# Dense feed-forward with up and gate units as seven block products, and modulation units 1024 columns wide

## The chip, the cores and the metric

The kernel runs on one core of one Trainium2 chip, in float32 throughout. The metric is the device time of one execution in microseconds (us). Engines are named as in the profile: PE is TensorE (matmuls), PEld its weight loads, DVE is VectorE, ACT is ScalarE, POOL is GpSimd, SP is SyncE, whose queue issues nearly all transfers.

## What is computed

256 tokens of width 1024 go through two layers of a first block (a mixer of three branches, then a feed-forward: dense in layer 0, eight experts in layer 1) and two layers of a second block. The change touches the dense feed-forward of layer 0 and the modulation vectors:

```python
D_MODEL, SEQ, D_FF = 1024, 256, 2816

def _swiglu(h, w1, w3, w2):
    return (jax.nn.silu(h @ w1) * (h @ w3)) @ w2

cond = jax.nn.silu(c)                       # 1024 numbers
for l in range(DEPTH):
    mod = cond @ w_mod[l] + b_mod[l]        # 6 vectors of 1024: sh1, sc1, g1, sh2, sc2, g2
    ...
    h = _modulate(_rmsnorm(x, norm2_w[l]), sh2, sc2)
    y = _swiglu(h, ffn_w1[i], ffn_w3[i], ffn_w2[i])    # layer 0
    x = x + g2[:, None, :] * y
```

## The kernel before

**Units and ring.** All weights come as a stream of units of 1 MB (128 partitions x 2048 numbers) into a ring of 11 slots in SBUF. SP issues the loads in the order of the stream; before each it waits until the unit that lay in that slot has been used: `unit_done` counts for units that PE uses, `part_done` for modulation units that DVE uses (L1400). A wait there holds back all later loads.

**Groups.** The 2816 hidden columns are 11 groups of 256 (`FG`, g = 0 to 10). PE's `swiglu` (L899) does, in group g >= 1: a `w1` unit and a `w3` unit through `columns_unit` (L492), each into one PSUM bank, transposed: 2 column blocks x 8 contraction blocks, with 128x128 of the weights stationary and all 256 tokens (`hT`) moving. Then `down(g - 1)` (L901) multiplies the hidden values of the group before by the `w2` unit into banks 4 to 7, which hold the sum of all groups. In some groups `mod_spread` (L575) follows, which turns a finished modulation vector. Group 0 goes through `lead_units` (L524), which works on the two token tiles apart, as their normed columns `hT` come in, with 128 tokens moving. Last comes group 10, with its own order.

**ACT** takes the `w1` bank through Silu into `gate_h[g % 2]` (L1781). **DVE** (`hidden`, L2526) multiplies that by the `w3` bank into `actT[g % 2]`, which PE's `down` needs. After it in its queue come, in group 0, `angles()` (L2074: masks and rotary angles for the second block, nothing near needs them), and in group g >= 1 the modulation units of `FFN_PARTS[g - 1]` (4 in group 1, 3 in groups 2 to 9), and `mod_spread` where a vector is complete. Every DVE instruction waits for the one before it (`link`).

**Banks.** `next_bank("U")` alternates banks 0 and 1, `next_bank("T")` banks 2 and 3. `free(bank)` makes PE wait until the last reader of that bank is done. 39 units have gone through "U" when group 0 starts, so its `w1` unit lies in bank 1 (read by ACT) and its `w3` unit in bank 0 (read by DVE).

**A modulation unit** is 1024 rows x 256 columns of `w_mod`. DVE's `row_product` (L2138) makes one `tensor_scalar` and seven `scalar_tensor_tensor` of 128x256 for it: acc = w * cond[k] + acc. Four units fill the 1024 columns of `PART[n % 2]`. 12 such units are spread over the mixer of layer 0 and 28 over the dense feed-forward.

**An existing scheme.** The mixer of layer 1 and the last stage already compute some 512-wide units with seven products instead of eight (`summed_product`, L1081): sums of weight blocks (DVE, `first_sums_in_place` and others) and of token blocks (`token_sums`, L2751), seven products, and partial results added on DVE (`added`, L2192). `SUMMED` says who reads each product.

Of the kernel before, what the change touches and what calls it, by code (L numbers as in the profile page):

```python
# [15 lines left out]
P = 128  # L16
# [178 lines left out]
def two_blocks(nc, stream, cols_d, rows_d, bgate_d, x_d, pos_d, out_d, stop=None):  # L195
# [3 lines left out]
    part_units = {(l, j): u for u, (name, l, j) in enumerate(names) if name == "part"}  # L199
    lead_at = {j: u for u, (name, l, j) in enumerate(names) if name == "lead"}  # L200
# [5 lines left out]
    with ctx:  # L206
# [173 lines left out]

        def by_k(a):
            return a.rearrange("p (k c) -> p k c", c=WC)

        D_T1 = [by_k(ring[:, RING_DSW, i * 2 * WC:(i + 1) * 2 * WC]) for i in range(2)]
# [15 lines left out]
        flatY = YT[:, :, :, :].rearrange("p b h s -> p (b h s)")  # L400
# [18 lines left out]
        def _(pe):  # L419
# [478 lines left out]

            def swiglu(l):  # L899

                def down(g, s=None, only=None):  # L901
                    if s is None:
                        s = landed_unit()
                    need(("w3", l, g))
                    for t in range(T) if only is None else only:
# [13 lines left out]
                for g in range(FG):  # L919
# [3 lines left out]
                    columns_unit("act", ("w1", l, g))  # L923
                    columns_unit("dve", ("w3", l, g))
                    if g < FG - 1:
                        down(g - 1)
                        for _ in FFN_PARTS[g - 1]:
                            skip_unit()
                        for part in parts_by[g]:
                            mod_spread(*part)  # L930
                        continue
# [627 lines left out]
        def _(act):  # L1559
# [221 lines left out]
            def swiglu(l):  # L1781
                for g in range(FG):
                    rows_out(("w1", l, g), gate_h[:, g % 2, :].rearrange("p (t c) -> p t c", t=T), ACT.Silu)
                    if g == 1:
                        angles()
# [203 lines left out]
        def _(dve):  # L1989
# [141 lines left out]
            def mod_part(l, j):  # L2131
# [4 lines left out]
                row_product(part_units[l, j], PART[n % 2][:, (j % 4) * UC:(j % 4 + 1) * UC])  # L2136
# [389 lines left out]
            def hidden(l, turn=None, dense=False, e=None):  # L2526
                for g in range(FG):
                    taken(("w1", l, g), turn)
                    b = bank_of(dve, ("w3", l, g), turn)
                    if dense:  # L2530
                        tt(actT[:, g % 2, :, :], view(b, 2, S), gate_h[:, g % 2, :].rearrange("p (k s) -> p k s", k=2),
                           ALU.mult, c=took)
                    else:
                        tt(actT_e[:, g % 3, :, :], view(b, 2, CAP), gate_e[:, g % 2, :, :], ALU.mult, c=took)
                    if dense and g == 0:
                        angles()
                    if dense and g == 1:
                        dve.wait_ge(*from_act.more())
# [21 lines left out]
                    if dense and g >= 1:  # L2560
                        for p in FFN_PARTS[g - 1]:
                            mod_part(*p)
                        for p in parts_by[g]:
                            mod_spread(*p)
# [123 lines left out]
            def ffn(l):  # L2688
                if l == 0:
                    hidden(l, dense=True)  # L2690
# [357 lines left out]
def lay_out(inp):  # L3048
# [9 lines left out]
    for u, (name, l, j) in enumerate(units):  # L3058
        if name in ("mod", "part", "lead"):
# [79 lines left out]
```

## Time and profile before

| | |
|---|---|
| three timed runs | 2308.69, 2308.86, 2311.12 us; median 2308.86 |
| profiled execution | 2313.64 us, of which span 2311.9 us |
| granted TensorE clock, mean over the span | 0.993 |
| PE busy | 2242.4 us (97% of the span) |
| DVE busy / ACT busy | 983.0 us (43%) / 478.6 us (21%) |
| dense feed-forward of layer 0 | about 397 to 640 us of the span |

A row of the timeline merges instructions of one form; a matmul of the program shows as two MATMUL and two LDWEIGHTS instructions, so that a `columns_unit` of 16 matmuls is 32. The duration of one MATMUL is longer than the distance to the next, since they overlap: PE's pace is the stretch divided by the count. "Idle before <- releaser" is the time in which the engine had nothing running, and what ended it. PEclk is the granted clock as a share of 2.4 GHz, 0.5 being 1.2 GHz.

### The profile page before, as it was taken

The page shows a single profiled execution, that of the slowest core. Times are in us where ns is not written, and L with a number is a line of the kernel's source. Part 1 is how long each engine was busy: PE and PEld are TensorE (multiplying, and loading weights), DVE is VectorE, ACT ScalarE, POOL GpSimd, SP SyncE. Part 2 cuts the span into 40 slices and gives each one's busy share as a digit, 9 for nine tenths or more (in the row PEclk, how much of TensorE's full clock was granted, in tenths as well). Part 3 has the DMA queues.
Part 4 walks back from the last instruction along what each step waited for, and adds up shares of the span by engine and source line. Part 5 has one row for each costly group of instructions (what it writes and reads, how often), then busy time and mean ns, then how long its engine had stood idle before and what let it go on. Part 6 is the DMA issues. An engine that isn't in the chain of part 4 may idle for free.

```text
span 2311.9 us, 48423 instructions
## 1 busy us (share of the span) xinstructions
PE 2242.4 (97%) x21380; PEld 1646.3 (71%) x21380; DVE 983.0 (43%) x2016; ACT 478.6 (21%) x889; POOL 26.7 (1%) x66
## 2 busy tenths in 40 slices
PE   8999999999999999989999999999999999999998
PEld 6888767777668876677877778777768874444544
DVE  3675642655563665331121121121123444475663
ACT  2343311000025332110000000000012431233343
POOL 2000000000000000000000000000000000000000
PEclk9999999999999999999999999999999999999999
DMA  9553255677533333549999999999982313343330
GB/s 377 191 215 141 91 218 201 241 287 304 205 128 128 130 127 125 212 175 399 401 403 408 395 403 399 397 408 401 408 328 110 110 64 137 127 146 124 114 109 19
DMA packets 75526, 537.96 MB, mean 233 GB/s; under 512 B 8552, under 2 KB 8560, under 8 KB 11440
## 3 DMA queue, kind: packets, MB, share of 16 engines
q1 hardware_dynamic: 72864, 526.14, 58.5%
q0 software_dynamic: 1360, 4.85, 0.6%
q8 instruction: 172, 2.82, 0.5%
q10 hardware_dynamic: 1088, 3.81, 0.4%
q14 instruction: 42, 0.34, 0.0%
HBM read 529.91 MB, written 4.85 MB: 231 GB/s over the span
## 4 chain that ended last, share of the span: by engine, by line
PE 91%; DVE 5%; ACT 3%; issue 1%; DMA 0%; DVEq 0%; ACTq 0%; SPq 0%
PE ps L956 21%; PE ps L487 11%; PE ps L476 11%; PE ps L1107 10%; PE ps L520 7%; PE ps L980 7%; PE ps L988 4%; PE ps L795 4%; PE ps L910 3%; PE ps L820 2%; PE ps L1210 2%; PE ps L564 2%; PE ps L1150 1%; PE ps L1341 1%; PE ps L1124 1%
## 5 line engine op out<-in xcount | busy, mean ns | idle before, releaser
L956 PEld LDWEIGHTS ps<-hT,ring 128*64 128x64 f32 x11264 | 474.5, 138 | 45.9 <-issue 41.5
L956 PE MATMUL ps<-hT,ring 128*64 128x96 f32 x11264 | 484.9, 247 | 6.2 <-DVEq L2742 4.2
L2007 DVE TENSOR_TENSOR RA<-ps,RA 128x192 f32<-128x192 f32 (+1 forms) x111 | 47.4, 427 | 665.3 <-PE ps L956 550.5
L1570 ACT ACTIVATE RA<-ps 128x192 f32<-128x192 f32 (+2 forms) x159 | 69.8, 439 | 1117.7 <-PE ps L956 574.4
L487 PE MATMUL ps<-hT,ring 128*128 128x256 f32 (+1 forms) x1280 | 269.0, 370 | 0.1
L476 PE MATMUL ps<-ring,hT 128*128 128x256 f32 x1184 | 262.0, 381 | 0.0
L487 PEld LDWEIGHTS ps<-hT,ring 128*128 128x128 f32 x1280 | 232.0, 190 | 33.1 <-issue 3.1
L476 PEld LDWEIGHTS ps<-ring,hT 128*128 128x128 f32 x1184 | 222.9, 190 | 31.7 <-issue 2.0
L520 PE MATMUL ps<-ring,hT 128*128 128x256 f32 x736 | 168.6, 384 | 2.0 <-DVE hT L2007 1.7
L980 PE MATMUL ps<-ring,RA 128*64 128x512 f32 x704 | 167.7, 594 | 0.1
L520 PEld LDWEIGHTS ps<-ring,hT 128*128 128x128 f32 x736 | 139.4, 193 | 22.6 <-issue 2.2
L1570 ACT ACT_TABLE_LOAD x86 | 110.3, 1283 | 55.4 <-DVE small L2013 28.2
L2007 DVE TENSOR_TENSOR ring<-ring 128x1024 f32<-128x1024 f32 (+3 forms) x101 | 106.1, 1050 | 25.3 <-ACT ring L1570 22.2
L1107 PE MATMUL ps<-ring,hT 128*128 128x512 f32 x216 | 97.5, 603 | 0.0
L988 PE MATMUL ps<-ring,RA 128*32 128x256 f32 x1408 | 85.9, 382 | 0.0
L980 PEld LDWEIGHTS ps<-ring,RA 128*64 128x64 f32 x704 | 46.4, 137 | 53.1 <-issue 53.1
L988 PEld LDWEIGHTS ps<-ring,RA 128*32 128x32 f32 x1408 | 40.8, 109 | 60.9 <-issue 38.9
L795 PE MATMUL ps<-ring,YT 128*128 128x512 f32 x192 | 83.1, 592 | 0.0
L1570 ACT ACTIVATE RB<-ps 128x512 f32<-128x512 f32 x60 | 35.8, 597 | 227.4 <-PE ps L476 94.5
L2016 DVE SCALAR_TENSOR_TENSOR QT<-ring,cond,QT 128x256 f32<-128x256 f32 x161 | 78.1, 485 | 5.8
L910 PE MATMUL ps<-ring,RA 128*128 128x512 f32 x176 | 77.5, 592 | 0.0
L1107 PEld LDWEIGHTS ps<-ring,hT 128*128 128x128 f32 x216 | 41.1, 193 | 49.6 <-issue 48.9
(327 smaller groups left out, 2164.8 us busy)
## 6 DMA issues: line engine op xcount, KB each, us to landing
ring<-stream SPq DMA_DIRECT2D x497, 1024.0 KB, 8.9
slots_scratch<-YT ACTq DMA_DIRECT2D x7, 384.0 KB, 8.4
x_rows<-x SPq DMA_DIRECT2D x2, 512.0 KB, 12.4
gates_row<-bgate SPq DMA_DIRECT2D x1, 1024.0 KB, 16.7
QT<-bgate SPq DMA_DIRECT2D x1, 1024.0 KB, 19.1
rows_scratch<-RB ACTq DMA_DIRECT2D x2, 512.0 KB, 4.7
out<-x_rows SPq DMA_DIRECT2D x2, 512.0 KB, 2.6
rowt<-rows SPq DMA_DIRECT2D x1, 460.0 KB, 14.1
```

The lines of the kernel that those rows point to most:

```text
L476: m = pe.matmul(ps[:, b, t * UC:(t + 1) * UC], lhs[:, k, t * P:(t + 1) * P], ring[:, s, k * UC:(k + 1) * UC], start=k == 0, stop=k == KC - 1)
L487: m = pe.matmul(ps[:, b, c * w + t * P:c * w + (t + tiles) * P], ring[:, s, k * UC + c * P:k * UC + (c + 1) * P], hT[:, k, t * P:(t + tile ...
L520: m = pe.matmul(ps[:, b, t * UC:(t + 1) * UC], hT[:, k, t * P:(t + 1) * P], ring[:, s, k * UC:(k + 1) * UC], start=k == 0, stop=k == KC - 1)
L795: m = pe.matmul(ps[:, b + t, :], YT[:, br, k, t * P:(t + 1) * P], ring[:, s, k * 512:(k + 1) * 512], start=k == 0, stop=k == 3)
L910: m = pe.matmul(ps[:, 4 + 2 * t + n, :], actT[:, g % 2, k, t * P:(t + 1) * P], ring[:, s, k * D + n * 512:k * D + n * 512 + 512], start=g ...
L956: m = pe.matmul(ps[64 * j:64 * (j + 1), b, c * CAP:(c + 1) * CAP], ring[:, s, k * UC + c * P + 64 * j:k * UC + c * P + 64 * (j + 1)], hT[: ...
L980: pe.matmul(ps[64 * j:64 * (j + 1), 4, :], actT_e[:, g % 3, k, 0:WIDE], ring[:, s, k * D + 512 * j:k * D + 512 * (j + 1)], **flags(g, k))
L988: m = pe.matmul(ps[32 * j:32 * (j + 1), 5, 0:256], actT_e[:, g_ % 3, k, WIDE:CAP], ring[:, s_, k * D + 256 * j:k * D + 256 * (j + 1)], **f ...
L1107: m = pe.matmul(ps[:, b, :], lhs, rhs, start=k == 0 and i in (0, 1, 3), stop=k == KH - 1, skip_group_check=i not in (0, 1, 3))
L1570: return nc.scalar.activation(out, in_, func, **kw)
L2007: link(v.tensor_tensor(out, a, b, op), c)
L2016: link(v.scalar_tensor_tensor(out, a, s_, b, op0, op1), c)
```

## The change

Three things change in the dense feed-forward, groups 1 to 10, and one in all modulation units of the kind `part`.

1. `columns_unit` is replaced by `column_product`. With the weights of a unit as 2x2 blocks (512 rows x 128 columns each) and the tokens as 2x2 blocks (128 tokens x 512), the four blocks of the result come from seven products (Winograd's form), i = 0 to 6, of 4 matmuls each, 128x128 stationary and 128 tokens moving. The `w1` and the `w3` unit take turns: product i of `w1`, product i of `w3`, product i + 1 of `w1` and so on. `w1` uses banks 0 and 1, `w3` banks 2 and 3; products 0, 2, 4, 6 go to the first bank of each and 1, 3, 5 to the second, most adding to what is there, so that each product waits until the result before it in its bank has been read.
2. DVE makes the sums: `token_sums("ffn")` once (4 `tensor_tensor` of 128x512), `column_sums` for the `w1` and the `w3` unit of each group (4 of 128x512 each, as soon as the last product of the group before is done), and adds three products per unit to the result (`added`, 128x128). ACT copies the other four products of each unit out of PSUM, and its Silu then works in place in SBUF.
3. DVE's order: per group g >= 1: `added` 1 (both units), from group 2 on one modulation unit, `added` 4 and 5, `column_sums(g + 1)`, the hidden product, `mod_spread`, in group 1 `angles()`, then the remaining modulation units (4 in group 1, 2 later). In group 0: token sums, column sums of group 1, hidden product.
4. A `part` unit is now 256 rows x 1024 columns, and DVE makes two instructions of 128x1024 for it instead of eight of 128x256.

```diff
@@ PE, column_product and swiglu @@
+            def column_product(key, s, b0, i):
+
+                b = b0 + (i in (1, 3, 5))
+                free(b)
+                if i == 2:
+                    pe.wait_ge(*sums.more())
...
+                for k in range(KH):
...
+                    m = pe.matmul(ps[:, b, 0:P], w[:, k, :], rhs, start=k == 0 and i in (0, 1, 3),
+                                  stop=k == KH - 1, skip_group_check=i not in (0, 1, 3))
...
-                    columns_unit("act", ("w1", l, g))
-                    columns_unit("dve", ("w3", l, g))
...
+                    at = [(name, landed_unit()) for name in ("w1", "w3")]
+                    for i in range(len(SUMMED)):
+                        for n, (name, s) in enumerate(at):
+                            column_product((name + "p", l, g), s, 2 * n, i)
+                    taken_by("act", [], ("w1", l, g))
+                    taken_by("dve", [], ("w3", l, g))
...
+                    if g < FG - 1:
+                        down(g - 1, s0, [0])
+                        for part in parts_by[g]:
+                            mod_spread(*part)
+                        down(g - 1, s0, [1])
+                        continue
@@ ACT, swiglu @@
+                for g in range(1, FG):
+                    for i, t, c in ((0, 0, 0), (2, 0, 1), (3, 1, 1), (6, 1, 0)):
+                        for name, dst in (("w1", gate_h), ("w3", F_UP)):
+                            b = bank_of(act, ((name + "p", l, g), i))
+                            link(fn(dst[:, g % 2, c * S + t * P:c * S + (t + 1) * P], ps[:, b, 0:P], ACT.Copy), took)
+                    taken((("w1p", l, g), 5))
+                    link(fn(gate_h[:, g % 2, :], gate_h[:, g % 2, :], ACT.Silu), took)
@@ DVE, mod_part @@
-                row_product(part_units[l, j], PART[n % 2][:, (j % 4) * UC:(j % 4 + 1) * UC])
+                s, fill, _ = plan[part_units[l, j]]
+                dve.wait_ge(landed[s], 16 * fill)
+                for i in range(2):
+                    k = j % 4 * 2 + i
+                    w = ring[:, s, i * D:(i + 1) * D]
+                    if k == 0:
+                        ts(PART[n % 2], w, cond[:, 0:1], None, ALU.mult)
+                    else:
+                        stt(PART[n % 2], w, cond[:, k:k + 1], PART[n % 2], ALU.mult, ALU.add, c=part if i else step)
@@ DVE, swiglu @@
+                def column_sums(name, g):
+                    s, fill, _ = plan[ffn_at[name, g]]
+                    dve.wait_ge(landed[s], 16 * fill)
+                    if g > 1:
+                        bank_of(dve, ((name + "p", l, g - 1), 6))
+                    t3, t2, t1, t4 = F_T[name]
+                    tt(t3, block_of(s, 1, 1), block_of(s, 0, 1), ALU.subtract)
+                    tt(t2, t3, block_of(s, 0, 0), ALU.add)
+                    tt(t1, block_of(s, 1, 1), t2, ALU.subtract)
+                    tt(t4, block_of(s, 1, 0), t2, ALU.subtract, c=sums)
...
+                for g in range(1, FG):
+                    parts = FFN_PARTS[g - 1]
+                    for name in ("w1", "w3"):
+                        added(name, g, 1, 0, 0, 0)
+                    if g > 1:
+                        for p in parts[:1]:
+                            mod_part(*p)
+                    for i, t, c, first in ((4, 1, 1, 3), (5, 0, 1, 2)):
+                        for name in ("w1", "w3"):
+                            added(name, g, i, t, c, first)
+                    if g < FG - 1:
+                        for name in ("w1", "w3"):
+                            column_sums(name, g + 1)
...
+                    hidden_of(g)
+                    for p in parts_by[g]:
+                        mod_spread(*p)
+                    if g == 1:
+                        angles()
+                    for p in parts[int(g > 1):]:
+                        mod_part(*p)
```

PE at the start of group 1, before: the last matmuls of group 0, then the two units (in the rows, `landed3` and `landed7` stand for the arrival of the units, `act_took` and `dve_took` for a bank read by ACT or DVE).

```order
L487 MATMUL ps<-hT,ring 128x128 x24
L487 MATMUL ps<-hT,ring 128x256 [waits act_took,landed3]
L487 MATMUL ps<-hT,ring 128x256 x15
L487 MATMUL ps<-hT,ring 128x256 [waits dve_took,landed7]
L487 MATMUL ps<-hT,ring 128x256 x15
```

And after, the first products of group 1; `sums_made` stands for the column sums.

```order
L500 MATMUL ps<-hT,ring 128x128 x24
L924 MATMUL ps<-hT,ring 128x128 [waits dve_took,landed7,landed3]
L924 MATMUL ps<-hT,ring 128x128 x3
L924 MATMUL ps<-hT,ring 128x128 [waits act_took]
...
L924 MATMUL ps<-hT,ring 128x128 [waits dve_took]
L924 MATMUL ps<-hT,ring 128x128 x3
L924 MATMUL ps<-YT,RA 128x128 [waits sums_made,act_took]
...
L924 MATMUL ps<-YT,RB 128x128 [waits sums_made,act_took]
...
L924 MATMUL ps<-YT,RA 128x128 [waits dve_took]
```

The first matmul of group 1 waited for a bank that ACT reads; now it waits for the bank that DVE's hidden product of group 0 reads.

DVE from the last `hT` columns to the first modulation unit, before.

```order
L2013 TENSOR_SCALAR hT<-ps,A,modc 128x128 [waits dve_took] x3
L2007 TENSOR_TENSOR RA<-ps,RA 128x512 [waits unit_done,act_took,dve_took]
L2077 TENSOR_SCALAR idx<-idx 128x256 [waits dve_took]
...
L2013 TENSOR_SCALAR sinr<-sinr 128x16 [waits dve_step]
L2007 TENSOR_TENSOR RA<-ps,RA 128x512 [waits unit_done,act_took,dve_gave_act]
L2011 TENSOR_SCALAR QT<-ring,cond 128x256 [waits burst_for_dve,landed9,act_gave_dve,dve_took]
L2016 SCALAR_TENSOR_TENSOR QT<-ring,cond,QT 128x256 [waits dve_step] x7
```

And after: from the last `hT` columns to the first partial result of group 1.

```order
L2053 TENSOR_SCALAR hT<-ps,A,modc 128x128 [waits dve_took] x3
L2047 TENSOR_TENSOR YT<-hT 128x512 [waits act_took,dve_took]
...
L2047 TENSOR_TENSOR RA<-ring 128x512 [waits landed3,dve_step]
L2047 TENSOR_TENSOR RA<-RA,ring 128x512 [waits dve_step]
L2047 TENSOR_TENSOR RA<-ring,RA 128x512 [waits dve_step] x2
L2047 TENSOR_TENSOR RB<-ring 128x512 [waits landed7,sums_made]
L2047 TENSOR_TENSOR RB<-RB,ring 128x512 [waits dve_step]
L2047 TENSOR_TENSOR RB<-ring,RB 128x512 [waits dve_step] x2
L2047 TENSOR_TENSOR RA<-ps,RA 128x512 [waits unit_done,act_took,sums_made]
L2047 TENSOR_TENSOR RA<-ps,RA 128x128 [waits act_took,burst_for_dve,dve_took]
```

The hidden product of group 0 (`RA<-ps,RA 128x512`) came right behind the columns; now four token sums and eight column sums stand ahead of it.

DVE at the end of group 1 and the start of group 2, after.

```order
L2047 TENSOR_TENSOR RA<-YT,RA 128x512 [waits act_took,sums_made]
L2117 TENSOR_SCALAR idx<-idx 128x256 [waits dve_took]
...
L2053 TENSOR_SCALAR sinr<-sinr 128x16 [waits dve_step]
L2051 TENSOR_SCALAR QT<-ring,cond 128x1024 [waits landed9,burst_for_dve,dve_gave_act]
L2056 SCALAR_TENSOR_TENSOR QT<-ring,cond,QT 128x1024 [waits dve_step]
...
L2056 SCALAR_TENSOR_TENSOR QT<-ring,cond,QT 128x1024 [waits landed5,part_done]
L2056 SCALAR_TENSOR_TENSOR QT<-ring,cond,QT 128x1024 [waits dve_step]
L2047 TENSOR_TENSOR RA<-ps,RA 128x128 [waits act_took,burst_for_dve,part_done]
```

The first partial result of group 2 that DVE reads (`RA<-ps,RA 128x128`) stands behind `angles()` and eight instructions of 128x1024; before, the hidden product of a group was the only one for which PE's next steps waited.

## Rows read from the trace of the kernel before

**Rows 1.** The page: busy time, and the chain that ended last.
```profile
PE 2242.4 (97%) x21380; PEld 1646.3 (71%) x21380; DVE 983.0 (43%) x2016; ACT 478.6 (21%) x889; POOL 26.7 (1%) x66
...
PE 91%; DVE 5%; ACT 3%; issue 1%; DMA 0%; DVEq 0%; ACTq 0%; SPq 0%
```

**Rows 2.** Windows, groups 1 to 10: length, busy (count) per engine, PEclk, DMA, GB/s.
```profile
413.60:630.70 217.10, 217.10 (x943) 158.23 (x943) 124.81 (x280) 7.89 (x14) 0.00 (x0) 1.00 0.69 273
```

**Rows 3.** Chain, groups 0 to 4: start us, us, what, instructions.
```profile
397.56 7.14 PE ps L487 x64
...
434.48 13.81 PE ps L487 x64
448.29 6.87 PE ps L910 x16
455.16 1.72 PE ps L581 x4
...
498.24 1.03 PE ps L587 x32
```

**Rows 4.** Timeline, PE, the start of `down(0)`: start us, us, instruction.
```profile
427.45 7.03 PE L910 MATMUL ps<-ring,RA 128*128 128x512 f32 x16
```

**Rows 5.** Groups of instructions with shapes apart, DVE and ACT: busy us, mean ns.
```profile
L2016 DVE SCALAR_TENSOR_TENSOR part_sum<-ring,cond,part_sum 128x256 f32<-128x256 f32 x140 | 67.9, 485 | 5.0
L2011 DVE TENSOR_SCALAR RB<-x_rows,small 128x1024 f32<-128x1024 f32 x12 | 9.0, 754 | 0.4
L2007 DVE TENSOR_TENSOR ring<-ring 128x512 f32<-128x512 f32 x12 | 8.3, 692 | 0.6 <-ACT ring L1570 0.2
L2016 DVE SCALAR_TENSOR_TENSOR ring<-ring 128x1024 f32<-128x1024 f32 x2 | 2.5, 1226 | 5.0 <-ACT ring L1570 5.0
L2120 DVE SCALAR_TENSOR_TENSOR junk<-ps,ident 128x128 f32<-128x128 f32 x10 | 2.9, 291 | 5.1 <-PE ps L610 4.8
```

**Rows 6.** Timeline, ACT and DVE around group 0, and layer 1's token sums.
```profile
405.68 1.93 ACT L1570 ACTIVATE hT<-ps,modc,A 128x128 f32<-128x128 f32 x4 [4.90 <-PE ps L564]
...
414.66 0.29 DVE L2077 TENSOR_SCALAR idx<-idx 128x256 int32<-128x256 int32 x1
...
422.74 0.17 DVE L2013 TENSOR_SCALAR sinr<-sinr 128x16 f32<-128x16 f32 x1
427.75 0.69 DVE L2007 TENSOR_TENSOR RA<-ps,RA 128x512 f32<-128x512 f32 x1 [4.83 <-PE ps L487]
...
650.36 0.69 DVE L2007 TENSOR_TENSOR part_sum<-hT 128x512 f32<-128x512 f32 x1 [0.70 <-ACT hT L1570]
651.08 0.69 DVE L2007 TENSOR_TENSOR part_sum<-part_sum,hT 128x512 f32<-128x512 f32 x1
```

**Rows 7.** Windows of 7 us, each from PE's first matmul after a wait.
```profile
269.40:276.40 7.00, 6.94 (x24) 6.04 (x25) 3.55 (x11) 4.22 (x9) 0.00 (x0) 0.60 0.02 7
635.90:642.90 7.00, 6.98 (x29) 4.76 (x30) 3.95 (x6) 1.83 (x4) 0.00 (x0) 1.00 0.00 0
...
865.90:872.90 7.00, 6.96 (x30) 6.17 (x31) 3.53 (x11) 4.22 (x8) 0.00 (x0) 0.79 0.03 11
1006.90:1013.90 7.00, 6.98 (x108) 6.98 (x110) 0.00 (x0) 0.33 (x1) 0.00 (x0) 0.62 0.05 15
```

**Rows 8.** Timeline, PE: the waits ahead of these windows [idle before <-releaser].
```profile
269.46 1.22 PE L769 MATMUL ps<-ring 128*128 128x256 f32 x2 [1.80 <-ACT ring L1570]
...
635.92 1.09 PE L564 MATMUL ps<-ident,RB 128*128 128x128 f32 x8 [1.83 <-DVE RB L2011]
...
865.93 1.22 PE L769 MATMUL ps<-ring 128*128 128x256 f32 x2 [1.80 <-ACT ring L1570]
...
1006.92 9.28 PE L956 MATMUL ps<-hT,ring 128*64 128x96 f32 x158 [4.15 <-DVEq L2742]
```

**Rows 9.** Windows, the mixer of layer 0 and after it.
```profile
80.00:120.00 40.00, 39.49 (x204) 33.96 (x203) 31.38 (x74) 17.21 (x40) 0.00 (x0) 1.00 0.63 237
120.00:160.00 40.00, 38.56 (x189) 32.63 (x188) 31.51 (x63) 16.49 (x26) 0.00 (x0) 1.00 0.62 237
```

More of the change, by code:

```diff
@@ L199, in two_blocks @@
     part_units = {(l, j): u for u, (name, l, j) in enumerate(names) if name == "part"}
+    ffn_at = {(name[:2], g): u for u, (name, _, g) in enumerate(names) if name in ("w1f", "w3f")}
     lead_at = {j: u for u, (name, l, j) in enumerate(names) if name == "lead"}
@@ L379, in two_blocks, with by_f, block_of @@
                 "mix": [S_TOP[:, 0], S_TOP[:, 1], S_MIX[:, 0], S_MIX[:, 1]]}
+        flatY = YT[:, :, :, :].rearrange("p b h s -> p (b h s)")
+        def by_f(a):
+            return a.rearrange("p (k c) -> p k c", k=KH)
+        def block_of(s, kh, c):
+            return ring[:, s, kh * KH * UC:(kh + 1) * KH * UC].rearrange("p (k c) -> p k c", k=KH)[:, :, c * P:(c + 1) * P]
         def by_k(a):
             return a.rearrange("p (k c) -> p k c", c=WC)
+        S_FFN = flatY[:, 0:2048].rearrange("p (i k s) -> p i k s", i=4, k=KH)
+        S_OF["ffn"] = [S_FFN[:, i] for i in range(4)]
+        F_UP = flatY[:, 2048:3072].rearrange("p (n c) -> p n c", n=2)
+        F_T = {name: [by_f(R[:, i // 2, 1024 + i % 2 * WC:1024 + (i % 2 + 1) * WC]) for i in range(4)]
+               for name, R in (("w1", RA), ("w3", RB))}
         D_T1 = [by_k(ring[:, RING_DSW, i * 2 * WC:(i + 1) * 2 * WC]) for i in range(2)]
@@ L2524, in mixer, with swiglu, added, hidden_of @@
                 project(f"m{l}o", f"n2{l}", A2_l[l], modc_l[l][:, 24:32], gates_l[l][:, 0, :])
-            def hidden(l, turn=None, dense=False, e=None):
+            def swiglu(l):
+                def added(name, g, i, t, c, first):
+                    key = (name + "p", l, g)
+                    b = bank_of(dve, (key, i))
+                    taken((key, first))
+                    a = (gate_h if name == "w1" else F_UP)[:, g % 2, c * S + t * P:c * S + (t + 1) * P]
+                    tt(a, ps[:, b, 0:P], a, ALU.add, c=took)
+                def column_sums(name, g):
[8 more added lines that the diff above has]
+                    tt(t4, block_of(s, 1, 0), t2, ALU.subtract, c=sums)
+                def hidden_of(g):
+                    taken(("w1", l, g))
+                    up = view(bank_of(dve, ("w3", l, g)), 2, S) if g == 0 else F_UP[:, g % 2, :].rearrange("p (k s) -> p k s", k=2)
+                    tt(actT[:, g % 2, :, :], up, gate_h[:, g % 2, :].rearrange("p (k s) -> p k s", k=2), ALU.mult, c=took)
+                taken((f"n2{l}", 1, 1))
+                token_sums("ffn")
+                for name in ("w1", "w3"):
+                    column_sums(name, 1)
+                hidden_of(0)
+                for g in range(1, FG):
[9 more added lines that the diff above has]
+                    if g < FG - 1:
+                        for name in ("w1", "w3"):
+                            column_sums(name, g + 1)
+                    if g == 3:
+                        dve.wait_ge(*from_act.more())
+                    hidden_of(g)
[5 more added lines that the diff above has]
+                        mod_part(*p)
@@ L2527, in hidden @@
+            def hidden(l, turn=None, e=None):
                 for g in range(FG):
@@ L2529, in hidden @@
                     b = bank_of(dve, ("w3", l, g), turn)
[L2530 to L2538, printed above, removed]
+                    tt(actT_e[:, g % 3, :, :], view(b, 2, CAP), gate_e[:, g % 2, :, :], ALU.mult, c=took)
                     if turn is not None and g == 0:
@@ L2689, in ffn @@
                 if l == 0:
-                    hidden(l, dense=True)
+                    swiglu(l)
                     mod_bias(1, 0, A1_l[1], "n1")
@@ L3058, in lay_out @@
     for u, (name, l, j) in enumerate(units):
-        if name in ("mod", "part", "lead"):
+        if name == "part":
+            stream[u] = unit_of(w_mod[l][j % 4 * 2 * P:(j % 4 + 1) * 2 * P], j // 4 * D, D)
+        elif name in ("mod", "lead"):
             stream[u] = unit_of(w_mod[l], j * UC)
```

34 lines of the change are left out of this document (14 added, 20 removed).

## The prediction

> **What bounds the kernel now.** I read the page first: PE is busy for 97% of the span and 91% of the chain that ended last is PE [rows 1]. The table of stretches over groups 1 to 10 of the dense feed-forward shows more than that: 217.10 us, in all of which PE is busy at a clock of 1.00, while DVE works 124.81 us and ACT 7.89 us [rows 2]. So in this stage only PE's own work counts, and every wait that the change puts into it adds in full. The chain cuts the stage up: two units take 13.81 us (64 instructions), `down` 6.87 us, a spread 1.72 or 1.03 us [rows 3]. The ten groups repeat this.
>
> **PE's work.** A pair of units now costs 14 products of 4 matmuls, 112 instructions with 128 tokens moving. The trace has this form: the lead of group 0 took 7.14 us for 64, 0.1116 us each [rows 3]. So a pair costs 112 x 0.1117 = 12.51 us instead of 13.81, saving 1.30 us, and ten pairs save 13.0 us. One eighth of the columns goes, but a matmul half as wide costs a little more than half: 0.1116 against 13.81 / 64 / 2 = 0.108 us. That half, 0.108, bounds the pace from below, with a saving of 17.2 us; I take 0.1117, from 64 instructions of exactly this form. It is the bound from above too: that lead had satisfied waits between its matmuls, as the products have, and they are in its pace.
>
> The Trainium skill ("TensorE: Matmul & The Clock Gate", section "Wait — 56ns, not 53.3ns?") gives a matmul a small fixed cost beside its columns, the same at every width. By its 2.5 ns, off 0.2158 us and added again after halving, the narrow pace would be 0.109 us (an estimate) and the saving 16 us. The lead shows 0.1116 [rows 3], about twice that fixed cost, and the sum goes by the lead.
>
> **DVE's new work, per group.** Column sums: 8 x 0.725 us (0.692 by the row, and 0.73 from start to start) = 5.8 us [rows 5, 6]. Six additions of 128x128 out of PSUM at 0.291 + 0.035 = 0.33 us [rows 5]. A modulation unit had one instruction of 0.35 and seven of 0.485 us, 4.0 us with gaps. A wide one is not in the trace. Bounds for 128x1024: 1.226 us, the row without a scalar per partition, and 1.29 us, the 0.485 of 128x256 plus 768 columns at the 0.267 us per 256 between rows of 128x1024 and 128x512 [rows 5]. I take 1.29, since the narrow form shows the dearer start: 2 x 1.325 = 2.65 us per unit, and 0.79 + 7 x 1.325 = 10.07 us for the four of group 1, whose first instruction is a `tensor_scalar` (0.754 us) [rows 5].
>
> **Steady groups, 3 to 10.** Take a group's first product as 0; a product lasts 0.894 us. The last `w1` product ends at 11.62. DVE starts 0.30 us behind, as it did behind the unit that ended when `down` began [rows 4, 6]: 11.92. Column sums to 17.73, hidden product to 18.46, two modulation units to 23.76. The next group starts at 12.51 + 6.87 = 19.38 or, with a spread, 1.03 to 1.72 later. So DVE is free 4.38 us into it and has the first addition of `w1` done at 4.70. PE needs that bank at its seventh product, 5.36. Slack 0.65 us: hidden, barely. The other waits (additions 4 and 5, ACT's copies, the sums at product 5) have over 2 us. Cost nothing; the cover is that 0.65 us. `down` needs a hidden product made a group earlier. The slots of units are freed at most some 10 us later than before and loads stay a group ahead of use at 273 GB/s [rows 2], so SP's queue costs nothing.
>
> **First wait: group 1.** The first product needs bank 0, and the order shows that its reader is DVE's hidden product of group 0, now behind twelve sums. ACT's `hT` columns end at 405.68 + 1.93 = 407.61 and DVE starts 0.10 later [rows 6]. Token sums 4 x 0.725: 410.61. Column sums 8 x 0.725: 416.41. Hidden product done 417.10, PE starts about 417.16. PE's group 1 started at 427.45 - 13.81 = 413.64 [rows 3, 4]. Wait: **3.5 us**. What is late next, the sums at the fifth product and the first addition, is ready by then.
>
> **Second wait: group 2.** Let F be the start of group 1. DVE does the sums for group 2 from F + 11.92 to F + 17.7, the hidden product to F + 18.5, then `angles()`, which took 414.66 to 422.91, 8.29 us with its gap [rows 6], then four units, 10.07 us: F + 36.8; the first addition of group 2 is done at F + 37.15. PE reaches its seventh product at F + 19.38 + 5.36 = F + 24.74. Wait: **12.4 us**. Before, the same work lay under 217 us of unbroken PE. With 1.226 instead of 1.29 us it is 12.0. Queued behind this wait is all of PE; DVE catches up meanwhile, and SP's held-back loads of group 3 (freed by these four units) still have over 10 us.
>
> **The clock.** After waits the granted clock is at 0.5 (1.2 GHz) for part of what follows. A window of 7 us with clock c lost 7 x (1 - c): 2.8 us after a wait of 1.80, 1.5 after another 1.80, 2.7 after 4.15, and nothing after one of 1.83 [rows 7, 8]. I take 1.7 us for the first wait, the mean of these four, with 0 to 2.8, and 2.7 for the second, by the longest wait of the four, with 1.5 to 2.8. Together 4.4 us.
>
> By the Trainium skill (the same page, section "The HAM clock gate") an idle PE falls to 1.2 GHz and work brings 2.4 GHz back. Three of the four rows agree, with 0.60, 0.79 and 0.62, and one does not, with 1.00 [rows 7]. By the rule alone each wait would be priced like the longest, 2.7 us, and the sum be 1.0 higher; by the rows it is as above.
>
> **Other places.** In the mixer of layer 0 twelve modulation units become 1.35 us shorter each on DVE. PE misses 0.5 and 1.4 us of the two stretches of 40 us in which eight of them lie [rows 9], so at most 1.9 us could return; the additions and copies around those waits are others', and I take 0. ACT gets eight copies per group, of about 0.3 us, and lies idle otherwise [rows 2].
>
> **Sum.** -13.0 + 3.5 + 12.4 + 4.4 = **+7.3 us**. Against its own execution that is 2311.9 + 7.3 = 2319.2 span and 2313.64 + 7.3 = 2320.9; that execution lies 4.8 us above the median, so the median becomes 2308.86 + 7.3 = **2316.2 us**.
>
> **Rivals.**
> - *The clock is not lost.* Place: the first 7 us after each wait. For it speaks the wait of 1.83 us with clock 1.00 behind it [rows 7, 8]; against it the other three rows, and that both new waits are longer than 1.8. Price: the sum falls to +2.9, 2311.8 us, not slower by what can be told; it decides from a loss under 1.7 us over both waits. Chance 0.12.
> - *DVE becomes the bound.* If the strided column sums take 0.80 instead of 0.692 us, 0.9 us is added ahead of the first addition, more than the 0.65 of slack: 0.2 us in each group without a spread, 0.9 in each of the first two waits, and PE stutters where the clock has suffered. Price 2 to 4 us: 2319.2 us. For it: the slack is small; against: 3D rows of the same size read `hT` at 0.69 us [rows 6]. Chance 0.13.
> - *The narrow pace is 0.109 us.* Then ten pairs of 112 x 0.109 = 12.21 us save 16.0, 3.0 more: 2313.2 us. For it: half of the wide pace is 0.108; against: the lead. The page on TensorE gives this pace, as said. Chance 0.08.
> - *The waits are shorter* (DVE gains in the mixer that PE feels, sums landing earlier, together 10 us or more). Faster, about 2303. For it I have only the 1.9 us above. Chance 0.05.
>
> **How the numbers follow.** A measurement of this kernel can tell about 0.2%, 4.6 us. The forecast has 0.62, and inside it the clock's bounds (1.5 to 5.6 us) give +4.4 to +8.5. With the bounds of 1.226 us (0.4 less) and 1.9 us from the mixer the low end is +2.1, with 3 us of the second rival the high end is +11.5: 2311.0 to 2320.4. That leaves out the faster case and the extremes of the others. Slower by over 0.2%: nearly all of the forecast (0.58), the second rival (0.13), half of the third (0.04): 0.75. Same: the first rival (0.12), the rest of the forecast (0.04) and of the third (0.04): 0.20. Faster: 0.05.
>
> **What the profile after would show.** Pairs of units of 12.5 us in the chain; PE idle some 3.3 us at 413.9 released by DVE's product of 128x512; PE idle some 12 us in the middle of group 2, released by a DVE addition of 128x128 behind eight wide instructions of 1.29 us; clock under 1.00 in both windows behind; no PE wait in groups 3 to 10. Wrong it would be if the narrow products ran at another pace, if the second wait were missing or shared by every group, or if the clock stayed at 1.00.

## The result, and the profile after

The changed kernel took 2319.82 us (median of five, 2319.19 to 2323.15), the kernel before 2310.2 us (median of five, 2308.69 to 2312.07). The ratio is 1.0045, 95% interval [1.003, 1.0059]. So it is slower, by 9.6 us, where no change lies outside the interval. The time lies inside the range that was given, near its upper end, 3.6 us above the forecast. Measured twice more, further down, the ratio was 1.0027 [1.0017, 1.0037] both times, which is +6.7 and +5.5 us. One of the nine executions of `e2_no_wait_2` took 3024.18 us at a mean granted clock of 0.719, and the table below leaves it out.

The page of the profiled execution (span 2319.3 us; the execution 2321.04 us), its rows of busy time and of the chain, which answer to [rows 1]:

```profile
PE 2234.4 (96%) x21860; PEld 1654.2 (71%) x21860; DVE 1005.6 (43%) x1920; ACT 501.1 (22%) x969; POOL 26.5 (1%) x66
...
PE 89%; DVE 6%; ACT 3%; issue 1%; DMA 0%; DVEq 0%; ACTq 0%; SPq 0%
```

PE is busy 8 us less (2242.4 before) in a span that is 7.4 us longer, and DVE has a larger share of the chain. PE's waits on DVE's additions and products, between 380 and 660 us (engine, line, who is waited for: us in total, times, longest):

```profile
PE ps L924 <- DVE RA L2047: 15.7, 2, 12.2
PE ps L577 <- DVE RB L2051: 1.8, 1, 1.8
```

The second row was there before. The first is new, and consists of two waits and no more. The timeline of PE shows them, with the idle time before the instruction in brackets:

```profile
415.11 5.38 PE L924 MATMUL ps<-hT,ring 128*128 128x128 f32 x32 [3.46 <-DVE RA L2047]
453.87 1.44 PE L924 MATMUL ps<-YT,RA 128*128 128x128 f32 x5 [12.22 <-DVE RA L2047]
```

The chain of work around them (start us, us, what, instructions), which answers to [rows 3]:

```profile
395.41 7.14 PE ps L500 x64
...
414.27 0.70 DVE RA L2047
415.11 13.44 PE ps L924 x104
...
434.48 0.70 DVE RA L2047
435.21 0.30 DVE idx L2117
...
443.50 0.77 DVE QT L2051
444.29 1.29 DVE QT L2056
...
452.21 1.30 DVE QT L2056
453.53 0.30 DVE RA L2047
453.87 10.02 PE ps L924 x64
...
472.48 12.51 PE ps L924 x112
...
645.60 6.91 PE ps L533 x32
```

The first wait ends with DVE's hidden product of group 0 (414.27), which has the column sums ahead of it. The second ends with the first addition of group 2 (453.53). Ahead of it the chain goes through the hidden product of group 1 (434.48), `angles()` (from 435.21) and the four wide units (443.50 to 453.5). A steady pair of units is the row of 12.51 us with 112 instructions, where it was 13.81 with 64 [rows 3].

From the start of group 0's lead to the start of layer 1's first product, the stage took 645.60 - 395.41 = 250.19 us. Before, it was 640.45 - 397.56 = 242.89. So the stage is **7.30 us** longer, and the forecast's sum was +7.3. The spans of the two executions differ by 7.4, so in this pair all but 0.1 us of the difference lies in the stage.

The clock behind the two waits, in windows of 7 us (columns as in [rows 2]; PEclk is the third last), and over groups 4 to 10:

```profile
414.99:421.99 7.00, 6.88 (x47) 6.91 (x48) 0.58 (x2) 0.83 (x3) 0.00 (x0) 0.76 0.12 49
453.76:460.76 7.00, 6.89 (x38) 6.89 (x39) 2.97 (x6) 0.55 (x2) 0.00 (x0) 0.60 0.58 235
492.00:634.00 142.00, 142.00 (x1028) 113.08 (x1027) 101.62 (x146) 21.41 (x65) 0.00 (x0) 1.00 0.75 297
```

The granted clock was at its lower level (1.2 GHz) for part of both windows. By the forecast's rule that is 7 x 0.24 = 1.7 us lost behind the first wait and 7 x 0.40 = 2.8 us behind the second. That an idle PE falls back to 1.2 GHz is also what the Trainium skill says ("TensorE: Matmul & The Clock Gate", section "The HAM clock gate"), and both windows agree with it. In groups 4 to 10 PE is busy all 142 us at 1.00.

### The profile page after: what moved, and what is told of

Same layout as the page of the kernel before. It is cut to its first block, busy times and chain, and to the rows that moved or that the text cites. A ratio compares the mean times of both kernels' runs of the same rounds, so it can differ in the third digit from the quotient of the medians.

```text
span 2319.3 us, 49538 instructions
## 1 busy us (share of the span) xinstructions
PE 2234.4 (96%) x21860; PEld 1654.2 (71%) x21860; DVE 1005.6 (43%) x1920; ACT 501.1 (22%) x969; POOL 26.5 (1%) x66
## 4 chain that ended last, share of the span: by engine, by line
PE 89%; DVE 6%; ACT 3%; issue 1%; DMA 0%; DVEq 0%; ACTq 0%; SPq 0%
PE ps L990 20%; PE ps L489 11%; PE ps L1141 10%; PE ps L533 7%; PE ps L1014 7%; PE ps L924 5%; PE ps L500 5%; PE ps L1022 4%; PE ps L808 4%; PE ps L941 3%; PE ps L833 2%; PE ps L1244 2%; PE ps L577 2%; PE ps L1184 1%; PE ps L1375 1%
## 5 line engine op out<-in xcount | busy, mean ns | idle before, releaser
L2047 DVE TENSOR_TENSOR RA<-ps,RA 128x192 f32<-128x192 f32 (+2 forms) x131 | 49.2, 376 | 615.4 <-PE ps L990 551.6
L1604 ACT ACTIVATE RA<-ps 128x192 f32<-128x192 f32 (+3 forms) x189 | 74.9, 396 | 1085.9 <-PE ps L990 574.6
L500 PE MATMUL ps<-hT,ring 128*128 128x256 f32 (+1 forms) x640 | 129.0, 360 | 0.1
L500 PEld LDWEIGHTS ps<-hT,ring 128*128 128x128 f32 x640 | 110.9, 190 | 14.7 <-issue 0.7
L1604 ACT ACTIVATE ring<-ring,small 128x256 f32<-128x256 f32 (+3 forms) x112 | 61.2, 547 | 68.9 <-DVE small L2915 55.2
```

The source lines that it names most:

```text
L500: m = pe.matmul(ps[:, b, c * w + t * P:c * w + (t + tiles) * P], ring[:, s, k * UC + c * P:k * UC + (c + 1) * P], hT[:, k, t * P:(t + tile ...
L1604: return nc.scalar.activation(out, in_, func, **kw)
L2047: link(v.tensor_tensor(out, a, b, op), c)
```

## The experiments

The theory: the products save 13 us, and two waits of the warm-up (groups 1 and 2), with the clock that each costs, eat that and more. Each wait is the order of DVE's work and not its amount. The rivals: DVE's wide units or its sums slow every group; the loss lies outside the stage; or the clock is lost, or kept, whatever the waits do.

The table gives, for every kernel, the difference of the medians to the kernel before on the same chip, the length of the stage (start of the lead, start of layer 1's product, from the chain of waits), its difference to 242.89, and PE's two waits. All lengths and waits are those of the one profiled execution of each row.

| kernel | us | against before | ratio [95%] | stage | stage against before | wait 1, wait 2 |
|---|---|---|---|---|---|---|
| after | 2319.82 | +9.6 | 1.0045 [1.003, 1.0059] | 250.19 | +7.30 | 3.46, 12.22 |
| e5_after_again | 2314.97 | +6.7 | 1.0027 [1.0017, 1.0037] | 249.01 | +6.12 | 3.47, 12.23 |
| e9_after_third | 2314.34 | +5.5 | 1.0027 [1.0017, 1.0037] | 249.20 | +6.31 | 3.46, 12.23 |
| e1_angles_early | 2307.55 | -0.4 | 1.000 [0.999, 1.001] | 241.08 | -1.81 | 3.47, 4.14 |
| e2_no_wait_2 | 2301.39 | -6.6 | 0.9977 [0.9966, 0.9987] | 235.08 | -7.81 | 3.47, none |
| e3_no_wait_1 | 2309.8 | +1.9 | 1.0011 [1.0, 1.0021] | 244.60 | +1.71 | none, 12.23 |
| e4_no_waits | 2296.05 | -11.9 | 0.9957 [0.994, 0.9973] | 229.83 | -13.06 | none, none |
| e10_no_waits_again | 2297.74 | -11.1 | 0.9954 [0.9941, 0.9968] | 229.83 | -13.06 | none, none |
| e6_wide_only | 2307.43 | -0.9 | 0.9998 [0.9988, 1.0008] | 242.89 | 0.00 | none, none |
| e7_keep_clock | 2314.75 | +6.5 | 1.0029 [1.0018, 1.0039] | 247.57 | +4.68 | 3.47, 1.86 |
| e8_narrow_units | 2334.1 | +25.3 | 1.0117 [1.0102, 1.0132] | 269.80 | +26.91 | 3.47, 18.33 and eight more |

### What the second wait consists of

The first experiment takes `angles()` out of the DVE queue ahead of it: all but its last instruction is moved to the end of layer 0's mixer.

```diff
                 else:
                     for j in range(16, 20):
                         mod_part(0, j)
+                    angles()
...
                     if g == 1:
-                        angles()
+                        angles_given()
```

> Only the mask and angle work of DVE (8.3 us) is taken out of group 1 and done while the gate units of the mixer of layer 0 run. Theory (wait 2 is DVE's queue of angles and four wide units, end to end): the wait in group 2 falls from 12.2 us by 8.3 to 3.9 us, the clock loss behind it stays between 1.5 and 2.8 us, so 8 to 9.5 us less than the changed kernel: 2311. Rival (the wait is about something else in group 1, such as the four units' loads or the sums): it stays near 12 us, 2320. Rival (cost only moves): DVE then delays the mixer's end by up to 8 us, visible as PE idle at 330 to 345 us, 2319.

Measured: the wait fell from 12.22 to 4.14 us, by 8.1 us, about what `angles()` took before (8.29). PE's timeline:

```profile
445.99 2.07 PE L924 MATMUL ps<-YT,RA 128*128 128x128 f32 x8 [4.14 <-DVE RA L2047]
```

The stage became 9.1 us shorter than in the changed kernel; the rest is what is lost behind the wait, 1.8 us here where it had been 2.9 (worked out below). So the wait was a queue of instructions on DVE, and `angles()` was two thirds of it. The cost did not move to the mixer: between 290 and 400 us PE's only wait on DVE is one of 1.6 us, as in the kernel before. Against the kernel before the total is 10.0 us lower than in the first measurement of the changed kernel and 5.9 to 7.1 lower than in its repeats; 8 to 9.5 had been expected.

The second experiment has that edit too, and puts two of group 1's four wide units between its first and its fourth additions, ahead of the column sums of group 2, where DVE waited for PE anyhow.

```diff
-                    if g > 1:
-                        for p in parts[:1]:
-                            mod_part(*p)
+                    for p in parts[:1 if g > 1 else 2]:
+                        mod_part(*p)
...
-                    for p in parts[int(g > 1):]:
+                    for p in parts[1 if g > 1 else 2:]:
                         mod_part(*p)
```

> As the run with the angles early, and of the four modulation units of group 1 two stand between the first and the fourth addition, two behind the hidden product, as in later groups. Theory: no wait in group 2 and no clock loss there, 12.2 + 2.75 = 15 us less than the changed kernel: 2305. The wait of 3.5 us in group 1 is still there. Rival (DVE is the bound in every group once the first is relieved): waits of 1 to 2 us spread over groups 2 to 10, about 2312.

Measured: no second wait; PE's only wait on RA is the first. In the chain group 1's pair and `down`, and group 2's pair, follow each other without a gap, and only the pair behind the first wait is longer, 14.29 instead of 12.50 us:

```profile
414.72 14.29 PE ps L924 x112
429.01 6.87 PE ps L941 x16
435.88 12.50 PE ps L924 x112
```

The kernel is now 0.23% faster than before (the ratio; the medians differ by 6.6 us). Nothing of PE's or DVE's work was taken away for it; it was only put in another order.

### The first wait alone

In the changed kernel each unit uses its two banks so that the first product of group 1 needs the bank that DVE's hidden product of group 0 reads. The third experiment swaps the banks of the units that begin with bank 0, and lets the hidden product go between the column sums of `w1` and `w3`.

```diff
-                b = b0 + (i in (1, 3, 5))
+                b = b0 + ((i in (1, 3, 5)) != (b0 == 0))
...
-                for name in ("w1", "w3"):
-                    column_sums(name, 1)
+                column_sums("w1", 1)
                 hidden_of(0)
+                column_sums("w3", 1)
```

> The two banks of each pair are swapped, so the first product of group 1 goes to the bank that ACT has read, and the hidden product of group 0 stands between the column sums of w1 and of w3. Theory: the wait of 3.46 us in group 1 and 1.7 us of clock loss go, the wait of 12.2 us in group 2 stays: 5.2 us less, 2314.6. Rival (the column sums themselves hold PE): a wait of some 2 to 3 us moves to the fifth product, 2318.

Measured: the first wait is gone, the second is what it was. What was lost behind it is gone too: the 104 instructions that took 13.44 us now take 11.63, so beside its idle time the first wait cost 1.81 us, clock and fresh start together (1.7 was forecast for the clock).

```profile
412.81 11.63 PE ps L924 x104
...
449.78 9.69 PE ps L924 x64
```

### Neither wait

The two edits together:

> Both edits together. Theory: groups 1 to 10 run without a PE wait, pairs of units in 12.5 us instead of 13.8, so 13.0 us less than the kernel before: 2297. If the remaining 2 to 3 us of the measured difference that the forecast missed sit outside this stage, this run is still 13 us below before only if those too are gone with the waits; if they stay it is 2299 to 2300. Rival (products cost more than their pace in the long run): 2303 or more.

Measured: the stage is 229.83 us, 13.06 shorter than before. The sum's first term was 13.0 for ten pairs at 12.51 instead of 13.81 us. From 410 to 615 us, so from group 1 into group 10, PE is busy without a break at clock 1.00, while DVE works 152 of 205 us:

```profile
393.93 7.14 PE ps L500 x64
...
402.09 8.08 PE ps L500 x64
410.17 12.51 PE ps L924 x112
422.68 6.87 PE ps L941 x16
```
```profile
410.00:615.00 205.00, 205.00 (x1425) 162.06 (x1424) 152.22 (x217) 30.40 (x94) 0.00 (x0) 1.00 0.73 289
```

This version beats both kernels: 0.9957 of the kernel before. As only four executions stood behind it, it was run again, last of all:

> Both waits taken away, once more, since the first measurement had only four executions. By the sum of the steps (ten pairs 1.30 us shorter, nothing added) 13.0 us less than before: ratio 0.9944. By the rival, that something outside the stage got dearer by 2 to 3 us in every kernel with the narrow products, 0.9953 to 0.9957, as first measured.

It gave 0.9954 [0.9941, 0.9968] with the same stage, 229.83 us. The two intervals hold both what the stage alone gives (0.9943) and a kernel that is 1 to 2 us longer outside it; this stays open.

The four kernels add up. Wait 1 costs the stage 235.08 - 229.83 = 5.25 us, wait 2 costs 244.60 - 229.83 = 14.77, and both 250.19 - 229.83 = 20.36, which is their sum within 0.4.

### The wide units

The kernel before with only the modulation units 1024 wide, in the mixer too:

> Only the modulation units are 1024 columns wide, the products are as before. Theory: DVE works about 40 x 1.35 = 54 us less, and PE waits for none of it: no change within 1.9 us, 2308 to 2311. Rival (the wide units delay or help something in the mixer of layer 0): a difference of 2 us or more, seen as PE idle there.

Measured: nothing. The ratio is 0.9998, the stage 242.89 us to the hundredth. DVE's work in the two windows of the mixer [rows 9] is 7.0 and 3.5 us less, and PE's is unchanged in one and 0.4 us less in the other, where a wait on DVE became 0.36 us longer:

```profile
80.00:120.00 40.00, 39.49 (x203) 34.02 (x203) 24.41 (x44) 17.28 (x40) 0.00 (x0) 1.00 0.63 237
120.00:160.00 40.00, 38.20 (x188) 32.28 (x186) 27.98 (x45) 16.50 (x26) 0.00 (x0) 1.00 0.62 236
```

One wide instruction takes 1285 ns; 1.29 us had been taken, the upper of the bounds 1.226 and 1.29:

```profile
L2016 DVE SCALAR_TENSOR_TENSOR QT<-ring,cond,QT 128x1024 f32<-128x1024 f32 x35 | 45.0, 1285 | 1.2
```

So alone they are worth nothing. The reverse experiment has the new products with the units as they were before:

```diff
-                s, fill, _ = plan[part_units[l, j]]
...
-                        stt(PART[n % 2], w, cond[:, k:k + 1], PART[n % 2], ALU.mult, ALU.add, c=part if i else step)
+                row_product(part_units[l, j], PART[n % 2][:, (j % 4) * UC:(j % 4 + 1) * UC])
```

> The products of the change as they are, but the modulation units narrow again (eight instructions of 128x256 each on VectorE, 4.0 us per unit, where the wide ones take 2.65). What the theory of the slack expects: the first addition of a group in steady state was 0.65 us ahead of PE's seventh product; two narrow units put 2.7 us ahead of it, so PE waits about 2.05 us in each of groups 3 to 10 that has no spread ahead of it, and 0.3 to 1.0 us in those that have one. The wait in group 2 grows by four units, 12.2 + 4 x 1.35 (and 0.6 for the first, cheaper instruction) = 17.6 to 18.2 us; the one in group 1 stays at 3.5. Without clock losses the stage is 6 + 8 to 13 us longer than in the changed kernel, with them up to 2.8 us more per wait: about 2330 to 2350 us. The rival, that VectorE has much more slack than was worked out or that the order of its work hides the units: only the 6 us of group 2 are added, about 2321 us, and groups 3 to 10 show no wait.

Measured: 2334.1 us, 25.3 more than before. The second wait is 18.33 us (17.6 to 18.2 had been expected), and each of groups 3 to 10 has a wait. In PE's timeline the first row is group 2's, and the others are those of groups 3 to 8:

```profile
457.75 2.08 PE L924 MATMUL ps<-YT,RA 128*128 128x128 f32 x8 [18.33 <-DVE RA L2047]
483.73 1.16 PE L924 MATMUL ps<-YT,RA 128*128 128x128 f32 x8 [1.70 <-DVE RA L2047]
505.33 1.16 PE L924 MATMUL ps<-YT,RA 128*128 128x128 f32 x8 [1.97 <-DVE RA L2047]
527.14 1.16 PE L924 MATMUL ps<-YT,RA 128*128 128x128 f32 x8 [0.95 <-DVE RA L2047]
548.95 1.16 PE L924 MATMUL ps<-YT,RA 128*128 128x128 f32 x8 [0.94 <-DVE RA L2047]
572.01 1.16 PE L924 MATMUL ps<-YT,RA 128*128 128x128 f32 x8 [1.70 <-DVE RA L2047]
593.62 1.16 PE L924 MATMUL ps<-YT,RA 128*128 128x128 f32 x8 [1.97 <-DVE RA L2047]
```

Behind a `down` without a spread the wait is 1.97 (2.05 had been expected), behind one with a spread of 1.03 us it is 0.94 or 0.95. Behind the spread of 1.72 us it is 1.70 where 0.3 had been expected, because DVE itself takes part in that spread, with two additions of 128x512, 0.70 us each, that the expectation had left out. The clock stayed at 1.00 in the 7 us behind each of these eight short waits, and was 0.56 behind the long one:

```profile
457.75:464.75 7.00, 7.00 (x36) 7.00 (x37) 4.46 (x11) 0.55 (x2) 0.00 (x0) 0.56 0.41 150
483.73:490.73 7.00, 7.00 (x62) 7.00 (x63) 5.53 (x14) 0.83 (x3) 0.00 (x0) 1.00 0.84 315
505.33:512.33 7.00, 7.00 (x62) 7.00 (x63) 5.53 (x14) 0.83 (x3) 0.00 (x0) 1.00 0.83 291
```

So the wide units are what keeps DVE off the path in the steady groups. Beside the new products they are worth 20.6 us in the stage (269.80 - 249.20, both on the same chip): 6.1 of it in the wait of group 2, 13.2 in the eight others with 0.26 us each to start again (worked out below), the rest behind the wait of group 2. Without the new products they are worth nothing.

### What the clock costs

To keep PE's clock up through the second wait, 24 products with a constant were put into it, ahead of group 2's seventh product. They write to columns of bank 0 that nothing reads, but the result of this kernel is wrong (relative error 0.80). The cause was not looked into, and only the time is read here.

```diff
                 b = b0 + (i in (1, 3, 5))
+                if key == ("w1p", 0, 2) and i == 3:
+                    free(0)
+                    for _ in range(24):
+                        pe.matmul(ps[:, 0, S:2 * S], ident[:, :], causal[:, :], start=True, stop=True)
                 free(b)
```

> The changed kernel with 24 matmuls of the identity (48 instructions of 256 columns, 10.4 us) added in the wait of group 2, into columns of a bank that nothing reads. Theory: the wait keeps its length, since DVE sets it, but the granted clock stays at 1.00 behind it, 2.75 us less than the changed kernel: 2317. Rival (the clock costs nothing that the wait does not cover): no difference, 2320. If DVE or its end moved with PE's activity, the wait would be longer.

Measured: PE now idles 1.86 us ahead of the first real product, which starts at the same time as in the changed kernel (453.84 and 453.87). The window behind it has clock 1.00, and the 64 instructions take 7.41 us:

```profile
453.84:460.84 7.00, 7.00 (x62) 7.00 (x63) 3.82 (x8) 0.83 (x3) 0.00 (x0) 1.00 0.70 260
```
```profile
453.84 7.41 PE ps L928 x64
```

In unbroken running 64 of them take 7.15 us (12.51 x 64 / 112). So this wait costs 0.26 us to start again, at full clock; the short waits of the previous experiment cost it too, e.g. 505.33 - 483.73 = 21.60 = 12.50 + 6.87 + 1.97 + 0.26. 0.16 us of it is a matter of counting: the idle time begins at the end of the last MATMUL, which lasts 0.27 us, where the next one would have started after 0.11. The other 0.10 shows in the first eight instructions, 1.16 us behind a wait where eight in the stream take 1.06. The clock costs the rest: after the second wait the same 64 took 10.02 us in the first execution, 8.78 and 8.97 in the two repeats, 9.69 in e3, and 8.98 behind the wait of 4.14 us. The loss over 7.15 is 2.87, 1.63, 1.82, 2.54 and 1.83 us. Less 0.26 for the start, the clock itself cost 2.6, 1.4, 1.6, 2.3 and 1.6 us, and 1.55 behind the first wait (1.81 - 0.26). The loss differs from one execution to the next behind the very same wait, and that is why the stage is 7.3, 6.1 and 6.3 us longer in three executions of one kernel.

The total did not follow: the ratio is 1.0029, against 1.0027 for the changed kernel on the same chip, though the stage is 1.4 us shorter (247.57 against 249.01). That is less than these measurements tell apart, so the clock's price is shown in the trace only, and the 2.75 us that had been expected is not found in the total.

### The same kernel again

> The changed kernel again, to size the difference. The profiled pair differs by 7.4 us (2321.04 against 2313.64), the timed medians by 9.6. Theory A (the sum of the forecast, 7.3, is the difference and the rest is the spread of the runs): 7 to 9 us over before. Theory B (2 to 3 us are lost outside the stage): 10 to 11 us over before, and the trace shows where.

> The changed kernel once more, because its two measurements gave 1.0045 and 1.0027, with intervals that hardly meet, and its profiled stage was 7.3 and 6.1 us longer. If the change is worth its stage alone, the ratio is 1.0025 to 1.0035 and the time outside the stage differs from that of before by as much as two runs of one kernel differ. If something outside the stage got dearer, the ratio is 1.004 or more and the trace shows the same place longer again.

Both gave 1.0027, beside stages that are 6.1 and 6.3 us (0.27%) longer. For e5 that is less than either theory had (7 to 9 or 10 to 11 us); e9 is where the stage alone would put it. The first measurement's 1.0045 isn't confirmed, though its interval [1.003, 1.0059] overlaps theirs.

What the eleven measurements have in excess of their stage (difference of the medians less the difference of the stage) runs from -1.6 us (e8) to +2.3 (after), with 0.7 as the mean: e6, whose stage is the same as before, has -0.9, and e4 and e10, which are one kernel, have +1.2 and +2.0. The span less the stage says how much the rest of the program varies by itself: 2069.0 us in the kernel before and 2069.1 in the changed kernel in the first pair, but 2065.5 and 2064.3 in the changed kernel's repeats (2314.5 - 249.01, 2313.5 - 249.20), and 2059.9 and 2062.7 in e4 and e10. So the rest of one and the same kernel differs by up to 4.8 us between two executions (the runs were spread over several chips), more than any of the excesses, and no cost outside the stage is shown. Between 75 us and the stage, PE waits longer than before in two places, by 0.36 us for DVE and by 0.4 for ACT, and e6 has both. What makes the rest vary is open.

## Where the prediction failed, and what held

**The step that failed** is the last one of the sum, from one execution to the median: "that execution lies 4.8 us above the median, so the median becomes 2308.86 + 7.3". The step before it held: 2313.64 + 7.3 = 2320.9 was forecast for the execution, and the profiled execution of the changed kernel took 2321.04. But this one lies only 1.2 us above its median of 2319.82, where 4.8 had been taken, and that difference is nearly all of the miss of 3.6 us. 1.3 us of it come from the median before, which rested on three executions and became 2310.2 with two more. The other 2.3 us are the excess of that measurement over the stage; in the two repeats the excess is +0.6 and -0.8. The prediction gave no width to this step, though its own rows had three times and a fourth from 2308.69 to 2313.64 us for one kernel. The term for the clock behind the second wait was mis-sized too, as said below.

**The mechanism held**: two waits in groups 1 and 2, with the clock behind them, outweigh what the products save. That the sum met the stage of the first execution to the hundredth is partly luck, as the repeats show.

- **What bounds the stage**: right. PE was saturated from group 1 to 10 [rows 2], and each wait came through in full: 5.25 and 14.77 us for the two, with what is lost behind them.
- **The products**: right. 12.51 us per pair, 13.06 us saved in the kernel without waits (13.0). The pace of 0.1117 us, taken from the lead [rows 3] and not from half of the wide one, holds, and so the third rival (0.109) falls.
- **First wait**: 3.46 to 3.47 us (3.5), released by the hidden product, as was said. That product starts 18.86 us behind the start of the lead (414.27 - 395.41), and 18.85 had been worked out (416.41 - 397.56).
- **Second wait**: 12.22 us (12.4), at the place and behind the rows that were named. The forecast reckoned both waits from start to start, which gives 0.16 us more than the idle time: 3.6 and 12.4 us. e1 takes `angles()` out of it and e2 the rest.
- **The clock**: behind the first wait 1.8 us were lost (1.7). Behind the second it was 2.9 us (2.7) in the first execution, 1.6 and 1.8 in the two repeats, so by the mean of 2.1 it was put too high by 0.6. Without the 0.26 us of the fresh start the clock alone took 1.55 us behind the first wait, and 2.6, 1.4 and 1.6 behind the second. The term was taken from the longest wait of four [rows 7, 8]; their spread of 1.5 to 2.8 was the better statement. The first rival, no loss, falls.
- **Steady groups**: no wait in groups 3 to 10, as was said. The slack of 0.65 us was too small. DVE's timeline for group 4:

```profile
490.76 0.75 DVE L2051 TENSOR_SCALAR QT<-ring,cond 128x1024 f32<-128x1024 f32 x1
491.55 3.93 DVE L2056 SCALAR_TENSOR_TENSOR QT<-ring,cond,QT 128x1024 f32<-128x1024 f32 x3
495.51 0.29 DVE L2047 TENSOR_TENSOR RA<-ps,RA 128x128 f32<-128x128 f32 x1
```

  and PE's row of the seventh product of that group:

```profile
497.05 1.06 PE L924 MATMUL ps<-YT,RA 128*128 128x128 f32 x8
```

  DVE goes on behind the addition at 495.84, so the slack is 1.21 us. One of the four wide instructions is a `tensor_scalar` of 0.75 us, which had been priced like the other three; that is 0.54 of the 0.56 us. Not every group has this instruction there: the least slack is 0.94 us, in group 3 (476.73 to 477.67), behind a spread of 1.72 us in which DVE itself works for about 1.45. The second rival falls: the column sums took 692 or 693 ns each, as priced, and the 0.9 us that it put in their way would just have been hidden in every group.
- **The mixer**: 0 taken, 0 found (e6).
- **The sum**: +7.3 forecast, +7.30, +6.12 and +6.31 in the stages of three executions.
- **The chances**: slower by over 0.2% had 0.75, and came. The forecast behind it was 0.32%; the repeats give 0.27%, nearer to the bound of 0.2% than the first measurement's 0.45%.

## What to carry to other kernels

When work moves from the engine that is the bound to one with time to spare, the average of that spare time says little: go through the other engine's queue in order, at the start of a stage above all, where one-time work lies (here 8 us of `angles()` and a double portion of units), and find the instruction that the bound engine needs from behind it. Such a wait can be cured by order alone: here three moves of DVE's work and a swap of two banks, with the same instructions, took the change from +0.3% to about -0.4%. An edit that is worth nothing alone, such as wider instructions on an idle engine, can be what carries the other one, so it is tested both without it and by itself.

## What the runs showed of the hardware

- Behind one and the same wait of 12.2 us, 1.4, 1.6, 2.3 and 2.6 us were lost to the clock in four executions (e5, e9, e3, after). Behind the eight waits of 0.94 to 1.97 us in e8, with some 20 us of unbroken work between them, the clock was 1.00 in the 7 us looked at. In the kernel before it was 0.60 and 0.79 behind two waits of 1.80 us [rows 7, 8], so the length of the wait alone does not decide it.
- Beside its idle time and the clock, a wait of PE cost 0.26 us to start again (e7, and the short waits of e8): 0.16 us of overlap with the MATMUL before, and 0.10 us in the first eight instructions.
- Outside the changed stage, one and the same kernel took up to 4.8 us more or less from execution to execution (after against e9). A stage that was 1.4 us shorter in the trace (e7 against e5) did not show in the medians of eight and ten executions.
- A `scalar_tensor_tensor` of 128x1024 with a scalar per partition took 1285 ns (e6); in the kernel before the form without that scalar took 1226 [rows 5].
